# Five order tables of a mixed decoder step with expert retrieval: the places of single units are set anew

## The reference, cut to what matters

```python
def peer_block(xt):                     # 128 tokens, 8 heads, 16 experts for each
    q = (xt @ w_q).reshape(128, 8, 2, 128)
    s1, s2 = scores of q[:, :, 0] and q[:, :, 1] against 128 sub-keys each
    top, ci = top_k(all sums of the 16 best of s1 and the 16 best of s2, 16)
    idx = e1 * 128 + e2                 # 16 of 16384 experts for a token and head
    g = softmax(top)
    act = gelu(einsum('thkd,td->thk', u_tab[idx], xt))
    return einsum('thk,thkd->td', g * act, v_tab[idx])
```

## Time and profile before

| what | value |
|---|---|
| median of 3 runs | 2215.53 us (2204.23 to 2223.11) |
| profiled execution | span 2207.0 us; what lies around the span is not given, and the span is 8.5 us under the median |
| busy share of the span | PE 69%, DVE 63%, POOL 55%, ACT 16% |
| bytes moved by DMA | 751.57 MB, mean 341 GB/s |
| gathers of expert rows | 528 of `u` and 528 of `v`, 937 ns the median issue on POOL |

### The profile page before, as it was taken

How to read it: one execution, slowest core, us unless ns; L and a number is a source line. 1 busy time by engine, 2 the same in 40 slices (tenths; PEclk the granted TensorE clock), 3 DMA queues, 4 the chain that set the end, 5 groups by cost and what they waited for, 6 DMA issues and landing times. The chain is left out here.

```text
span 2207.0 us, 25764 instructions
## 1 busy us (share of the span) xinstructions
PE 1531.2 (69%) x9198; PEld 745.6 (34%) x9198; DVE 1395.3 (63%) x3469; ACT 355.5 (16%) x901; POOL 1212.1 (55%) x1097
## 2 busy tenths in 40 slices
PE   5676446865546879977687889968778850555567
PEld 2345113541123426533532437525423310111112
DVE  1447988599875655558498836499687327443641
ACT  0100112111112211013131201122223110111111
POOL 0004377545777574437475754467675438745774
PEclk8687778987877979888796888977887785578658
DMA  9719899998989899898798998989998889999998
GB/s 366 276 47 403 291 374 335 413 362 329 384 323 370 297 417 419 341 364 315 274 347 316 315 362 345 377 324 338 363 339 302 323 317 338 380 419 419 335 350 310
DMA packets 213942, 751.57 MB, mean 341 GB/s; under 512 B 27236, under 2 KB 35628, under 8 KB 213816
## 3 DMA queue, kind: packets, MB, share of 16 engines
q0 software_dynamic: 155136, 564.20, 68.4%
q1 hardware_dynamic: 58680, 185.72, 21.6%
HBM read 747.74 MB, written 2.10 MB: 340 GB/s over the span
## 5 line engine op out<-in xcount | busy, mean ns | idle before, releaser
L779 POOL DMA_INDIRECT uring<-in_peer_u,expert x512 | 580.6, 1134 | 511.5 <-DVE dots L1932 211.0
L1217 PE MATMUL yacc<-vring,diag 64*64 64x512 f32 x4096 | 653.6, 738 | 229.9 <-DMA vring<-in_peer_v,expert 163.2
L779 POOL DMA_INDIRECT vring<-in_peer_v,expert x512 | 556.4, 1087 | 425.8 <-PE yacc L1217 290.4
L1932 DVE CUSTOM_DVE_ANT_0 uring<-uring,h 128x1024 f32<-128x1024 f32 x512 | 615.3, 1225 | 161.4 <-DMA uring<-in_peer_u,expert 144.1
L1217 PEld LDWEIGHTS yacc<-vring,diag 64*64 64x64 f32 x4096 | 155.2, 156 | 610.0 <-DMA vring<-in_peer_v,expert 338.8
L1453 ACT ACTIVATE diag<-cst,wts 128x64 f32<-128x64 f32 (+1 forms) x528 | 172.9, 344 | 868.7 <-PE yacc L1217 630.0
L1005 PE MATMUL pp<-hT,wring 128*128 128x128 f32 x992 | 132.3, 294 | 21.7 <-issue 15.9
L1005 PEld LDWEIGHTS pp<-hT,wring 128*128 128x128 f32 x992 | 125.8, 208 | 35.4 <-issue 29.6
L1805 DVE TENSOR_REDUCE arena<-arena 128x16 f32<-128x1024 f32 x64 | 77.8, 1215 | 28.6 <-ACT arena L1392 27.7
L1706 DVE MAX8 t<-sc 128x8 f32<-128x128 f32 (+1 forms) x68 | 19.9, 292 | 117.5 <-ACT sc L1253 83.2
L1068 PE MATMUL pq<-w_uk,arena 128*128 128x512 f32 x128 | 74.6, 672 | 22.9 <-ACT arena L1392 22.9
(11 more groups left out here) (301 smaller groups left out, 1854.0 us busy)
## 6 DMA issues: line engine op xcount, KB each, us to landing
wring<-in_peer_w_q SPq DMA_DIRECT2D x47, 1024.0 KB
wring<-in_w_mod SPq DMA_DIRECT2D x38, 1024.0 KB
wring<-in_sg_w_in SPq DMA_DIRECT2D x48, 768.0 KB
wring<-in_sg_w_out SPq DMA_DIRECT2D x18, 1024.0 KB
wring<-in_mla_w_o SPq DMA_DIRECT2D x9, 1024.0 KB
uring<-in_peer_u,expert POOLq DMA_INDIRECT x512
vring<-in_peer_v,expert POOLq DMA_INDIRECT x512
uring<-in_w_mod SPq DMA_DIRECT2D x6, 1024.0 KB, 16.7
```

The source lines that it names most:

```text
L779: pool.indirect_dma_start(ring[:, slot % RING, :], None, table[n // 3], bass.IndirectOffsetOnAxis(ap=idx, axis=0)).then_inc(land[slot % RI ...
L1217: last = pe.matmul(yacc[64 * q:64 * q + 64, r], diag[at, slot % RING, :], v[at, 512 * q:512 * q + 512], start=first, stop=final)
L1932: dve.tensor_tensor_reduce(u, u, rows_h[:, :], 1.0, 0.0, ALU.mult, ALU.add, dots[:, p % 2, i:i + 1]).then_inc(u_used, 1)
```

## The change: the five tables are written anew

The change replaces the text of the five tables. The fixed work, the steps, the rings and the numbers of units are the same (528 U and V, 528 D, 34 T, P and W on DVE, 4 Y, 183 weight chunks, 8 K, 8 C), and so are the bytes. Units move to other spots one by one and in short runs. Since the tables take six lines more, line n of before is line n+6 of the changed kernel. Two lines of each of two tables:

```diff
 PLAN_PE = """
-189:VVVVVVVVVVVVVVVV 197:VVV 199:V 200:VVVVV 207:V 208:VVVVVV 213:VVV 217:VV 218:V 232:V 237:VV 239:V 260:VV 280:V
...
+182:VV 189:VVVVVVVVVVVVV 196:V 197:V 198:VV 199:V 200:V 202:V 203:VV 207:V 208:VVVV 209:VVV 213:VVVV 217:V 218:V 221:V
...
 PLAN_POOL = """
-UUUUUUUUVVUVVVVVUUUUUUUUUUUUUUUVVUVVVVUUVVVUVVVVVUVUUUUUUUUUUVVVUUUUUUUVVVVVVVUUUUUUVVUUVUUUUUVVUUVUUUUUUUVUUUUVUVUV
...
+UUUVUUVVUUUUUUVUVUUUUUVUVUVVUVUUVVVUUVUVVUUVVVVVUUUVUUUUUUUUUUUVUUVUVVUUVVVVUVUVUVUVUUVVUUVUUVUUUUUUUUVUUVUUUUUVUUUV
...
```

More of the change, by code:

```diff
@@ L124 @@
+919:V 923:V 924:V 926:V 927:VVVVVV 929:V 936:V 938:V 941:VVVVVVVVV 943:VVVVVVV 946:VVVV 949:V 950:V 953:V 964:VVVVVVVV
+965:V 967:V 968:VV 976:V 987:VVV 990:V 994:V 995:VVV 1001:V 1005:V 1006:VV 1008:VV 1009:V 1013:VVVVVVVVVVVVVVV
+1020:VVVVVVVVV 1022:V 1024:VV 1030:V 1042:VVVVVVVVVV 1073:VVV 1076:V 1083:VV 1091:VVVVV 1096:V 1097:VV 1099:V 1100:VV
+1101:VVVVV 1103:VVVVV 1106:V 1107:V 1108:V 1109:VV 1116:V 1120:VV 1122:VVV 1124:VVVVVV
+1127:VVVVVVVVVVVVVVVVVVVVVVVVVVVVVVVVVVVVVVVV 1131:VVVVVVV
 """
@@ new lines @@
+1041:W 1042:UU 1044:UUU 1051:UU 1060:UU 1062:U 1066:UUUU 1074:U 1081:PU 1082:U 1083:UUW 1090:U 1098:U 1108:U
+1112:UUUUUU 1115:U 1123:U 1127:UP 1130:W 1154:U 1156:U 1163:U 1165:U 1178:UUUUUUUU 1179:U 1193:U 1207:UUP 1214:W
+1215:UUUU 1218:U 1219:UU 1246:U 1255:U 1286:U 1299:U 1314:U 1318:U 1326:U 1330:UU 1332:PWUUUU 1334:UUUU 1337:UU 1338:U
+1363:UU 1369:UU 1377:U 1387:UU 1394:PUWUU 1399:U 1424:U 1438:UU 1442:U 1444:U 1447:U 1450:U 1453:UU 1457:UUPU
+1460:UUUW 1468:U 1485:UU 1486:U 1488:U 1494:U 1499:UU 1531:U 1533:U 1535:U 1556:PU 1562:U 1567:W 1593:U 1595:UU
@@ L172 @@
-516:WWWWWWWWWW
+0:WWW 1:WWW 5:WW 10:WW 16:W 23:WWW 30:WWWW 32:WWW 37:WWWWW 40:WW 41:WWWWWWWW 53:WWWWWWWWWWWWWWWWWWWWWWW 115:WWWW
+117:WWW 124:W 134:WWWWWW 142:WWWWW 143:WW 185:W 222:WW 224:WW 226:W 233:WW 236:W 240:W 242:W 257:WWWWWWWW 261:W
+269:WWWWWWWWWWWWWW 325:W 348:WWWWWWWW 351:W 359:WW 360:W 368:WWWWWWWWWWW 377:WW 381:W 385:WWWWWWWWWWWWW 397:WWW
+455:WWW 464:WWW 465:W 474:W 500:WWW 503:W 508:WW 511:W 516:WWWW 517:WW 518:W 521:WWWW
 """
```

93 lines of the change are left out of this document (43 added, 50 removed).

## The result

| | before | changed |
|---|---|---|
| median (range), first chip, 4 runs each | 2214.1 us (2204.23 to 2223.11) | 2262.76 us (2248.06 to 2288.49) |
| ratio | | 1.0212 [1.0147, 1.0277] |
| span of the profiled execution | 2207.0 us | 2250.7 us |
| ratio on two other chips, 6 runs each | | 1.0289 [1.025, 1.0328]; 1.0282 [1.0243, 1.0321] |

The account below looks back on a forecast made before the run. The stream of DMA transfers was taken as the bound, the span being its work plus idle DMA time: 2207.0 - 23.2 - 10 + 3 + 3 + 2 = 2181.8 us of span, so 2190 us; range 2150 to 2240.

Parts of the forecast that it names:

- the three places: Idle DMA holes at cache 3's latents and the mixes of tiles A and B: 23.2 us won, bounds 0 and 23.2.
- Cache 3's latents: POOL's wait for cache 2's "pv": nine gathers moved ahead of it fill the idle DMA time, 9.0 us won.
- The mix of tile B: V276 to V279 ahead of PE's mix let POOL issue later gathers sooner, 7.5 us won.
- The mix of tile A: One more unit ahead of the mix and two between its groups close the DMA hole, 6.8 us won.
- The small holes: Eight more windows of low DMA share, 37 us idle together: 10 us won, bounds 0 and 37.
- (a): PE stalls at D231 to D241, D360 behind route exps, and at early V0, V1: 3 us lost, bounds 0 and 62.
- (b): Up to 24 more U dots on DVE ahead of the sample's last route: 3 us lost, bounds 0 and 12.
- (c): SP issues 14 weight chunks instead of 8 ahead of the constants' loads: 2 us lost, bounds 0 and 15.
- (d): Gathers of C4 to C7 stand up to 17 gathers later, covered by 39 us of slack: cost 0.
- The slower case: PE stands at diagonals behind the exp, the full 62 us less 23.2 won: 2254 us, chance 0.17.
- no change: Holes close where they were and open elsewhere, the rings' limits being the same: 2215 us, chance 0.22.
- The byte limit: Memory's bytes bound the stretches, so only the hole at cache 3 is won: 2206 us, chance 0.03.

Follow-up runs that it names:

- e9: The kernel before with only units around the two SGU mixes moved ahead of them and cache 3's latents ten gathers further back: 1.0039 [1.0019, 1.0059].
- e7: The kernel before with the new places in steps 111 to 145 only (tile B's SGU and route, caches 5 to 7): 0 to 0.4% slower.
- e11: The kernel before with the new places in steps 0 to 43 only (start to tile B's norm): 0.9991.
- e1: The changed kernel with steps 71 to 93 (tile A's SGU) from before: 1.029 [1.0243, 1.0338] against the kernel before.
- e6: The kernel before with the new places in steps 94 to 110 only (tile A's layer 1 route, caches 2 to 4): 1.0084 [1.0052, 1.0116].
- e10: The kernel before with the new places in steps 172 to 176 only (the sample's last norm, query and route, last outputs): 0.9% slower.
- g1: The changed kernel once more, on one chip beside its version with the old tail: 1.0282 [1.0243, 1.0321] against the kernel before.
- g2: The changed kernel with steps 170 to 176 from before: 1.0265 [1.0223, 1.0307] against the kernel before.
- f1: The kernel before with new places in steps 94 to 110, but ACT's D185 to D191 ahead of and between the exps: 1.0045 [1.001, 1.008].
- e3: The kernel before up to step 93, the changed kernel's places from step 94 to the end: 1.0221 [1.0185, 1.0257].

## Why the prediction was wrong

**The failed step is the first one of the sum, the 23.2 us of the three places**, taken at their upper bound, **together with a term that the list of losses put at nothing**: the waits that the same rings get at new places. The two mixes alone give nothing (e9, 0.4% slower), and the stretch of tile A's SGU, with the new waits of V153, V160 and U203, costs 37 us. The premise that a wait of POOL costs what the DMA engines stand idle in its window covers 31 of the 47 us between the two ends of the transfers, and not the other 16. Point by point:

- *Cache 3's latents, 9.0 us.* The wait of 11.35 us is gone: both latents follow the gather ahead of them with 0.30 us between. These 9 us may well be won: the hole lies in the stretch of 300 to 375 MB, which is 20 us faster. No run shows it apart, since the other chips do not have the hole. (The keys behind these latents in the list of before are those of cache 4; the keys of cache 3 stood further up.)

```profile
1108.97 0.94 POOL L798 DMA_INDIRECT kv<-in_cache_kv,page_rows  x1 [0.30 <-issue]
1110.21 1.31 POOL L798 DMA_INDIRECT kv<-in_cache_kv,page_rows  x1 [0.30 <-issue]
```

- *The mix of tile B, 7.5 us.* The share is 1.03 in 1359 to 1376, so the hole is closed. POOL still stands there, for 10.52 us (V) and 10.91 us (U), and V288 waits 21.8 us further down. Alone it is worth nothing or less than nothing (e9; in e7 with all else of steps 111 to 145).

```profile
1359.67 2.82 POOL L785 DMA_INDIRECT vring<-in_peer_v,expert  x1 [10.52 <-PE yacc L1223]
...
1375.88 1.68 POOL L785 DMA_INDIRECT uring<-in_peer_u,expert  x1 [10.91 <-DVE dots L1938]
```

- *The mix of tile A, 6.8 us.* I looked at the seven units around PE's mix and not at the U dots that DVE's table moved out of the same mix, nor at the units ahead of the SGU's first transposes. Both opened larger waits (16.2, 11.8 and 22.3 us) than the one that was closed (8.66). With e9, which doesn't have these, the term still comes out as a loss: the two mixes, with cache 3's latents moved where they cost nothing, make the kernel 0.4% slower. For the mixes the bound "0, where the hole only moves" was the truth, and even it was not low enough.
- *The small holes, -10 us.* The DMA share from 163 to 1816 went from 0.92 to 0.91. Over the whole span the idle time by the packets went from 208 to 239 us: +31 where -33 was forecast. (The eight windows have shares up to 0.49, not 0.55 as the prediction says; their sum of 37 us is right.) The other 16 us of the 47 between the two ends of the transfers are busy time of the DMA engines for the same bytes, which the premise had no room for; fewer gathers out at a time fits them (the table above), but no run gives that alone.
- *(a) Diagonals behind an exp, +3 us.* The places I named are harmless. The transposes of cache 4's part ran at 1232.87, 66 us later than in the earlier trace rows, and the cache's first matmul at 1240.07, 30.7 us later, no more than the 38 us by which this cache's latents are issued later. V0's wait of 18 us costs nothing (e11). A place I had not named, D185 behind three exps, is real: 14.57 us of PE in e1 and e6 and perhaps half of the 0.8% of e6. In the changed kernel it is 8.01 us.
- *(b) The end, +3 us.* The mechanism was right, and so was its shift: 61 us worked out, 58 to 70 measured (that one pair of runs gives 61 is luck). The wait is there in the changed kernel, too. It was mis-sized: alone the last steps cost 0.9%, 19 us (e10), since behind the late route both last stretches take longer, beyond the wait of 8 us. In the changed kernel the exchange of the same steps is worth 0.17 points (g1, g2), with a new wait at the seam.
- *(c) The start, +2 us.* The share in 0 to 163 us is 0.61 for 0.62, and e11 shows the start to cost nothing.
- *(d) Cache gathers further back, 0 us.* Those of cache 7 were in time. But cache 5's latents, one of the gathers that I took to be covered, now wait for cache 4's "pv" with 7.1 us of idle DMA, which they did not before. The hole ahead of cache 3 is to be found again two caches on:

```profile
1304.05 0.94 POOL L798 DMA_INDIRECT kv<-in_cache_kv,page_rows  x1 [7.26 <-PE ps L1112]
```

- *The rivals.* The slower case was put at 2254 us, near 2263, but for another reason: PE at diagonals behind the exps of caches 3 and 6, which did not stall it. So its number is no credit. The case for "no change" had the mechanism: "the holes close where they were and open elsewhere". What it lacked is that they open longer than they were. The byte limit and "more gain" are out.

**What the runs support.** The rings give POOL seven gathers of slack of each kind, and one in-order list for both kinds. As the gathers that are out run down, first the bytes per second fall and only then the share, so a long wait should cost more than as much waiting in short pieces (read from the table; no run varied the length of waits alone). The new order has gathered units into runs, and seven waits over 10 us became sixteen. Each part that adds a wait with idle DMA (44 to 70, 71 to 93, 94 to 110, the last steps) costs about 1% alone; the parts that put one such wait for another (0 to 43, 111 to 145, and e9) cost 0 to 0.4%. What one wait costs beyond its idle time is not shown: e6 as a whole costs 17 us, with some 12 idle at V192, but without that wait (f1) only about 8 of them go. The costs don't add, for two reasons that the traces show: a delay that costs time alone is partly covered where transfers are late anyway (PE's wait at V185 is 14.6 to 14.9 us in e1, e3 and e6 and 8.01 in the changed kernel), and a splice has waits of its own (V192, V450). How much of the difference these make is not shown. All this is shown for parts; for a single unit only in e9 and f1, and there for a few units together.

**What stays open.** Which unit in steps 44 to 70 does it, and what the last steps, which cost 0.9% alone, cost in the changed kernel, where the wait of 8.85 us for the route is there too: no run takes it away without the wait of V450. No run gives tile A's old order to the changed kernel without the wait of V192, either, so the 2.1 to 2.9% are not divided among the causes. Why two groups of chips differ by 6% for the same kernel, spread over most of the span, while the fully fed stretch of 650 to 700 MB takes 119 us on the first chip and on the fast ones. On a fast chip (e11) some 380 us are spent with three or fewer gathers out, where the kernel before on the first chip spends over 700. How much of the 16 us of busy time is the number of gathers out. A larger ring was not tried.

No kernel of these beat the one before; the nearest is e11 at 0.9991.

## What to carry to other kernels

When an in-order engine issues for two consumers, a wait that is removed hands on to the next limit of the same cause: before a hole is counted as a gain, follow the issuing list beyond it to the first gather that needs a unit behind the same fixed step on any engine, and price that one. Judge a new order by the number and length of its long waits and by the transfers out at each moment, not by the profile's sums of waits by releaser or the share of the DMA engines alone, and look at every table that moved at the place, since one engine's gain was undone here by another's.

Prices of parts measured alone are not prices in the whole: here 4.3% of parts made 2.9%, and undoing a 1% part gave nothing back. Before a splice is read, look in its trace for a long wait that neither of the two kernels has: e1, e3, e6 and g2 each have one.

## What the hardware showed that was not expected

The mean busy share of the DMA engines is full (0.98 to 1.01) with four to five gathers of 512 KB out, and the rate still goes from 365 to 417 GB/s with six; above six it stays. Holding the kernel at four costs 9.4%. And the same kernel took 2085 to 2089 us on three chips and 2210 us on a fourth (2214 where it was first run), while the mean granted clock of two profiled runs near it differs little (0.80 in e11 at 2081.67 us, 0.79 in f1 at 2210.04 us).
